# A two-layer transformer block with 64 experts on one core: in the last layer, rows reach the experts and return by matrix products on chip

## What is computed

```python
def moe_ffn(h, router_w, router_bias, w_gu, w_down, shared_gu, shared_down):
    scores = jax.nn.sigmoid(jnp.dot(h, router_w))
    _, idx = lax.top_k(scores + router_bias, TOP_K)                # 6 of 64 experts for each token
    gates = jnp.take_along_axis(scores, idx, axis=-1)
    gates = gates / jnp.sum(gates, axis=-1, keepdims=True) * ROUTED_SCALE
    ...
    # for each expert e, on the rows of the tokens that chose it:
    #   y = (silu(rows @ w_gu[e][:, :384]) * (rows @ w_gu[e][:, 384:])) @ w_down[e]     times the gate
    return routed + swiglu(h, shared_gu, shared_down)
...
xl = xl + mod_l[5] * y
```

## Time and profile before

| what | before |
|---|---|
| median of 3 runs | 2591.6 us (2590.67 to 2595.17) |
| the profiled execution's span, first to last instruction | 2591.4 us |
| experts of the last layer: first weight transfer issued | 1766.44 us |
| span left after the stretch in which the transfers run without a break | 2535 us to the end |
| TensorE busy | 2249.8 us (87%) |
| DVE, ACT, GpSimd busy | 740.5, 417.0, 311.3 us |

### The profile page before, as it was taken

The page is one execution under the profiler, slowest core; times in us unless marked ns, Lnnn a source line. Parts: engine busy times, 40 slices in busy tenths (PEclk is TensorE's granted clock), DMA queues, the critical chain, the costliest instruction groups (busy, mean ns, idle before and its releaser), DMA issues. The chain is left out here.

```text
span 2591.4 us, 40524 instructions
## 1 busy us (share of the span) xinstructions
PE 2249.8 (87%) x17039; PEld 1151.1 (44%) x17039; DVE 740.5 (29%) x1653; ACT 417.0 (16%) x886; POOL 311.3 (12%) x368
## 2 busy tenths in 40 slices
PE   6999899999778797888888999898978889888887
PEld 2457644454333343434434557655433334343333
DVE  2365655371011011111115466645201101011112
ACT  2322344110000000000001333431000000000000
POOL 0007200011111111110000007100111101000000
PEclk8999999999989999999999999999998999999999
DMA  8000297279999999999988100136999999999994
GB/s 326 33 17 35 92 377 291 115 286 394 426 424 406 421 409 419 417 416 383 397 356 343 41 31 6 71 117 259 373 426 414 417 415 421 417 418 412 416 419 198
DMA packets 96345, 780.92 MB, mean 301 GB/s; under 512 B 21736, under 2 KB 22136, under 8 KB 37280
## 3 DMA queue, kind: packets, MB, share of 16 engines
q1 hardware_dynamic: 74848, 740.46, 69.7%
q0 software_dynamic: 21312, 37.81, 3.9%
HBM read 772.55 MB, written 41.29 MB: 314 GB/s over the span
## 5 line engine op out<-in xcount | busy, mean ns | idle before, releaser
L1513 PE MATMUL banks<-arena,htreg 128*32 128x384 f32 (+2 forms) x5824 | 879.4, 533 | 199.6 <-DMA arena<-in_exp_w_gu 194.3
L1513 PEld LDWEIGHTS banks<-arena,htreg 128*32 128x32 f32 (+2 forms) x5824 | 403.4, 137 | 648.7 <-issue 507.3
L1538 PE MATMUL banks<-arena,modreg 128*32 128x512 f32 (+2 forms) x2184 | 400.0, 598 | 40.5 <-issue 37.8
L2314 DVE TENSOR_TENSOR modreg<-modreg,banks 128x384 f32<-128x384 f32 x74 | 40.9, 553 | 1029.8 <-ACT modreg L1831 1029.8
L1538 PEld LDWEIGHTS banks<-arena,modreg 128*32 128x32 f32 (+2 forms) x2184 | 137.6, 127 | 250.4 <-issue 247.8
L1064 PE MATMUL banks<-arena,htreg 128*128 128x512 f32 (+3 forms) x480 | 159.0, 490 | 0.0
L2466 DVE COPY modreg<-banks 128x512 f32<-128x512 f32 x68 | 47.0, 691 | 318.9 <-PE banks L1538 318.9
L1837 ACT ACTIVATE modreg<-banks 128x384 f32<-128x384 f32 x74 | 36.3, 490 | 550.5 <-PE banks L1529 550.5
L2629 POOL DMA_INDIRECT y_d<-modreg,lst x68 | 67.5, 992 | 455.4 <-DVE modreg L2466 454.5
L1064 PEld LDWEIGHTS banks<-arena,htreg 128*128 128x128 f32 x480 | 89.7, 191 | 65.0 <-issue 61.0
L1831 ACT ACTIVATE modreg<-banks 128x384 f32<-128x384 f32 x74 | 36.3, 490 | 491.5 <-PE banks L1513 491.5
(11 more groups left out here) (407 smaller groups left out, 2173.6 us busy)
## 6 DMA issues: line engine op xcount, KB each, us to landing
arena<-in_exp_w_gu SPq DMA_DIRECT2D x256, 1536.0 KB
arena<-in_exp_w_down SPq DMA_DIRECT2D x128, 1536.0 KB
arena<-in_w_mod SPq DMA_DIRECT2D x32, 1024.0 KB, 11.4
arena<-y_d SPq DMA_DIRECT2D x6, 3072.0 KB, 16.7
modreg<-in_w_mod SPq DMA_DIRECT2D x14, 1024.0 KB, 8.3
modreg<-mod_d SPq DMA_DIRECT2D x20, 512.0 KB
arena<-in_shared_w_gu SPq DMA_DIRECT2D x6, 1536.0 KB
arena<-in_w_in SPq DMA_DIRECT2D x4, 2048.0 KB, 12.5
```

Of the source, the lines that this page charges most:

```text
L1513: last = mm(gu_bank(n, half)[rows, 0:DE], src[:, k, rows], up4[q][:, i, DE * half:DE * (half + 1)], start=(k == 0), stop=(k == KD - 1))
L1538: last = mm(ps[4 + half][rows, :], actT[:, k, rows], dn3[q][:, k, 512 * half:512 * half + 512], start=(k == 0), stop=(k == KE - 1))
L2314: tt(act_, sgb, gu_bank(n, 1)[:, 0:DE], ALU.mult).then_inc(unit_act.sem, 1)
```

## The change

In the last layer, nothing of a unit's rows passes through HBM any more. `places` holds for each token and each of the 100 groups of 32 slots the slot that the token has there; comparing it with 0..31 gives a one-hot matrix (`one_hot`), and the product of the token rows with it gives the unit's rows, already transposed (`gather_by_product`). The results return by the product with the transposed one-hot matrix, scaled with the gates (`gate_rows`, `gates_of`, `combine`), which DVE adds to an accumulator of all 256 tokens (`added`). The lists, the gathers, the scatters and the final reading of `y_d` go. Experts of few tokens share a unit by fours (32 slots each); there are 25 routed units (`LAST_CAPS`: 4 experts may have 128 slots, 4 have 96, 16 have 64 and 40 have 32). The second pass stays for rows beyond these slots, and is skipped as a whole when there are none. The first layer keeps its way.

```diff
+LAST_CAPS = ((4, 4), (4, 3), (16, 2), (40, 1))
+    whole = [[(u, i) for i in range(4)] for u in range(4)]
+    big = [[(u, 0), (u, 1), (u, 2), (67 - u, 0)] for u in range(4, 8)]
+    pair = [[(r, 0), (r, 1), (r + 1, 0), (r + 1, 1)] for r in range(8, 24, 2)]
+    quad = [[(r + i, 0) for i in range(4)] for r in range(24, 60, 4)]
...
+            for i, quad in enumerate(units[3]):
+                order.append(quad)
+                if i < 4:
+                    order += [units[0][i], units[2][i]]
+                elif i < 8:
+                    order += [units[1][i - 4], units[2][i]]
...
+                        experts[n] = [sp.value_load(eid[0:1, eid_at[l][r]:eid_at[l][r] + 1], min_val=0, max_val=NE - 1)
+                                      for r in WORK[l][n][1]]
...
+                def gather_by_product(n):
...
+                    for k in range(KD):
+                        for j in range(2):
+                            rows = h[:, 2 + j, :].rearrange("p (d k) -> p k d", k=KD)
+                            last = mm(ps[k // 4][:, tok(k % 4)], rows[:, k, :], hot[r % 2][:, j, :], start=(j == 0), stop=(j == 1))
+                def gate_rows(n):
...
+                    for i in range(4):
+                        column = perm[:, 4 * u + i:4 * u + i + 1].broadcast_to([NE, 32])
+                        last = mm(gu_bank(n, 0)[32 * i:32 * i + 32, :], column, by_expert, start=True, stop=True)
+                def combine(n, j):
...
+                    for half in range(2):
+                        if j and n < NW[l] - 1:
+                            pe.wait_ge(comb_added.sem, comb_added.at(0, 4 * r + half + 1))
+                        mm(comb_bank(n, j, half), gated[r % 2][:, P * j:P * j + P], outs[r % 2][:, 512 * half:512 * half + 512],
+                           start=True, stop=True).then_inc(comb_psum.sem, 1)
...
+                    for n in range(EARLY, NW[l] + 1):
+                        if n < NW[l]:
+                            unit_part(n, "lo")
+                        act_transposed(n - 1)
+                        if n > EARLY:
+                            gate_rows(n - 1)
+                        if n < NW[l]:
+                            unit_part(n, "hi")
+                        if n >= EARLY + 2:
+                            combine(n - 2, 0)
+                        if n + 1 < NW[l]:
+                            gather_by_product(n + 1)
+                        if n >= EARLY + 2:
+                            combine(n - 2, 1)
+                        unit_down(n - 1)
...
+                        tt(gated[r % 2], gated[r % 2], bank[:, SEQ:2 * SEQ], ALU.mult).then_inc(gated_ready.sem, 1)
...
+                            tt(acc_last[:, j, cols], acc_last[:, j, cols], gu_bank(n + 1, half)[:], ALU.add).then_inc(comb_added.sem, 1)
...
+                if l == LAST:
+                    more_last(pool, pool_more, zeros_and_lists)
+                    break
```

More of the change, by code:

```diff
@@ L369, in build @@
         RING = 4
[L370 removed]
+        eid = sb("eid", [P, max(NE, N_COL)], U32)
         lst1 = sb("lst1", [P, max(UNITS)], U32)
@@ L719, in heads4, with more_last, meet @@
             return ap.rearrange("p t (g d) -> p t g d", d=d)
+        def more_last(eng, body, before=None, after=None):
+            n_phase = phases["last"]
+            met = [n_phase - 1]
+            def meet():
+                met[0] += 1
+                eng.drain().then_inc(phase_done.sem, 1)
+                eng.wait_ge(phase_done.sem, 5 * met[0])
+            l = LAST
+            eng.wait_ge(addr_ready.sem, addr_ready.at(l, 1))
+            big = eng.value_load(maxcnt[0:1, 0:1], min_val=0, max_val=NT * P + P)
+            with eng.If(big > P):
+                meet()
+                if before:
+                    before()
+                meet()
+                with eng.Fori(0, R[l]) as r:
+                    with eng.Fori(0, NE // RING) as i:
+                        for b in range(RING):
+                            body(EX[f"more{l}"], l, r, RING * i + b, r * NE + RING * i + b,
+                                 r * (NE // RING) + i, b)
+                if eng is nc.gpsimd:
+                    done = EX[f"more{l}"]["scattered"][0]
+                    eng.wait_ge(done.sem, done.at(l, NE * R[l]))
+                meet()
+                if after:
+                    after()
+                meet()
+            eng.nop()
         def more_slots(eng, name, l, body, gives):
@@ new lines, in _ @@
+                dve.wait_ge(h_ready.sem, h_ready.at(2 * l + 1, n_t))
+                link(dve.memset(mask[:, n_t, :], 0.0))
+                dve.wait_ge(order_act.sem, order_act.after(l, "scores"))
+                link(tt(selb[:, nt_, :], scores[:, nt_, :], bc(srow("rbias"), 1, n_t), ALU.add))
+                for i in range(n_t):
+                    link(dve.max(out=top8[:, i, :], in_=selb[:, i, :]))
+                    link(dve.max_index(out=idx8[:, i, :], in_max=top8[:, i, :], in_values=selb[:, i, :]))
@@ new lines, in _ @@
+                link(ts(unit_hot[lo64, 0:U_], K("experts")[lo64, 0:U_], rankcol[lo64], None, ALU.is_equal))
+                dve.wait_ge(order_psum.sem, order_psum.after(l, "rank"))
+                link(dve.tensor_copy(rank, ps[0][:, 0:NE]))
+                link(ts(shift_by, rank, float(U_), 2.0, ALU.is_ge, ALU.mult))
+                link(stt(shift_by, rank, float(NE - G_), shift_by, ALU.is_ge, ALU.add))
+                link(ts(cap, rank, float(W_), 1.0, ALU.is_lt, ALU.add))
+                for end in (W_ + G_, NE - G_):
+                    link(stt(cap, rank, float(end), cap, ALU.is_lt, ALU.add))
```

575 lines of the change are left out of this document (399 added, 176 removed).

## The result

| | before | changed |
|---|---|---|
| median | 2593.1 us (4 runs, 2590.7 to 2595.2) | 2572.1 us (4 runs, 2570.4 to 2574.8) |
| profiled execution's span | 2591.4 us | 2570.5 us |
| ratio of the times | | 0.992, 95% interval 0.991 to 0.994 |

The change made the kernel 21 us faster, 0.8%. The forecast was 79 us, and its range (2494 to 2548) doesn't hold the result.

A forecast was written before the change was run, and what follows sets the result against it. The prediction took weight transfers to bound the last layer, with PE hidden: flow from 1771.3, plus 720 of stream, 5 of gaps and 16.2 of end, gives 2512 us, 79 less than before; range 2494 to 2548.

The forecast's parts named there:

- PE in a unit: PE's work per routed unit of the last layer: 22.8 us, some 24.5 with hand-overs; 25 units 610 us, hidden under 720.
- Does the ring hold?: Weight buffers of the last layer: PE needs about 42 us against 43, so they hold by a hair; 5 us of gaps.
- tight round: First half of the last layer's order: four-, one- and two-expert unit in turn, four times, with some tenths of gaps each.
- Rival 2: PE's chain in the last layer: two-sided hand-overs make a unit 28 us instead of 24.5; 2544 us, chance 0.10.
- The stream's price: Last layer's weight transfers: 3.75 us for each chunk of 1.573 MB, so 720 us for all 192 chunks.
- The bound from the end's slices: Last layer's weight transfers running alone at 427 GB/s: 3.68 us a chunk, 707 us for the layer.
- Rival 1: Last layer's weight transfers: row traffic was free, so a chunk keeps 3.93 us; 2546 us, chance 0.09.
- Rival 5: Last layer's weight transfers: alone they run at 427 GB/s without gaps, 707 us for 725; 2494 us, chance 0.10.
- The start: Start of the last layer's weight stream: first issue at 1769.2, flow from 1771.3, 2.8 us later than before.
- The end: From the last weight chunk to the kernel's end: 16.2 us in place of 55.4.
- Rival 3: PE in the last layer: clock stays at 1.2 GHz, a unit takes about 42 us; about 2850 us, chance 0.03.
- Rival 4: After the last layer's units: the second pass runs all 64 experts again; about 3950 us, chance 0.02.

The follow-up runs named there:

- e1: Changed kernel with the last layer's h written so that gathering products load contiguous columns, not every eighth value; same result: 2520.4 us, 0.973 of before.
- e3: Changed kernel with each unit's 16 gathering products replaced by eight transposes of contiguous rows, so units work on wrong rows: 2500.1 us, 0.965 of before.
- e4: Kernel before the change, its last layer's indirect gathers and scatters letting only the first row or two through: 2545.4 us, 0.982 of before.
- e8: Changed kernel with contiguous gathering loads and, in each round, the two-expert unit moved to directly behind the four-expert unit: 2513.7 us, 0.970 of before.

## Why the prediction was wrong

**The step that failed** is "PE in a unit". It set the new products at "16 products of the same 128x128 form (0.144 each: 2.3)", the gate rows at 0.45 and the four return products at 1.8, in all 22.8 us a unit, "some 24.5 with six hand-overs". Measured is 28.3 to 28.6 without its waits, 28.4 in what follows. With it failed the step that was built on it, "Does the ring hold?", which puts PE's work in a tight round at 42 us. Two errors made the new products 8.0 us too cheap:

- *Counting.* I took the mean of one record and multiplied it by the number of instructions in the program. But the trace shows each float32 product as two records. The evidence stood in front of me: the down part of a unit in four groups has 48 records in the timeline, where the order of the changed kernel lists 24 products for such a part. Return products are 3.8 us and not 1.8, gate rows 1.06 and not 0.45, and the gathering would be 32 x 0.117 = 3.7 us even without a stride. The Trainium skill, "FP8 and Floating Point Precision", section "TensorE Precision Notes", says that true FP32 needs four passes. The trace agrees in total: a record of 512 columns takes 0.44 us (5.31 / 12 in L1701, at a granted clock of 1.00, 2.4 GHz), so two records are some four cycles a column for one product.
- *The wrong neighbour.* The row of 0.144 us was that of transposes. They had the same stride of every eighth value and hardly showed it; a product does. e1 shows what the stride costs there: 0.239 against 0.117 us a record, 3.9 us a unit. The Trainium skill, "Advanced Engine Details and Errata", section "SBUF Cachelines", states that SBUF has lines of 16 bytes and that access to another line each time pays a penalty. Here the values lie 32 bytes apart, and the trace agrees that there is a penalty; the page gives no figure, and that the lines are its reason is not shown by any run here.

Half of this error was hidden by luck. The other terms were too dear: `lo` and `hi` at 6.1 us each ran at 5.4 (1.5 us), and of the 1.7 us of hand-overs nothing is seen, the groups even overlap by 0.9 us in all. So 24.5 + 8.0 - 1.5 - 1.7 - 0.9 = 28.4.

**Why a unit of 28.4 us costs so much.** 25 x 28.4 = 710 us is still less than the 720 of the stream as forecast (at 3.69 us a chunk it is 708), so by means alone PE would be nearly hidden. But the ring is only eight chunks deep, and units differ in weights, not in PE time. A round of three units takes PE 85.4 us, waits and the slower parts behind them left out. In the first four rounds it needs 21 chunks, 78 us at e3's price: PE sets the pace. In the later ones 24 chunks, 89 us: the stream should. The stretches between the first and the fifth, and the fifth and the eighth four-expert down part:

```profile
1843.56:2202.53 358.97, 348.26 (x1941) 195.07 (x1940) 76.22 (x133) 18.96 (x36) 0.00 (x0) 0.98 0.90 373
2202.53:2484.64 282.11, 263.74 (x1780) 139.88 (x1780) 57.06 (x100) 14.23 (x27) 0.00 (x0) 0.95 0.97 405
```

The first four rounds take 89.7 us each, in place of the forecast's 21 x 3.75 = 78.8: 44 us lost in four rounds, with the DMA share at 0.90. The next three take 94.0 in place of 90: another 12. Together 56, about the 57 us by which the last weights come later than forecast (about 2553 for 2496). In every round PE also waits once, at the four-expert unit, for 2 to 6 us, and then runs one `hi` part in 6.6 to 8.1 us in place of 5.4. So both lose: neither is busy throughout, and the sum is longer than either alone.

The forecast's own check of the ring shows the 11 us of a tight round, once it has the measured parts. It puts the last down part of a four-expert unit 42 us behind the start of its `hi` part, against 43 us of transfers. In the timeline above the `hi` part starts at 2065.34 and the down part ends at 2117.91: 52.6 us, since the products and the gathering, taken as 4.7 us, are 11.1 and 11.0. All transfers that the ring allows are done by then. The DMA rate from 2060 to 2140 us (2 us a slice) is 0 from 2110 to 2118, and SP sends the next chunk when the down part ends:

```profile
GB/s 418 424 455 399 442 438 406 418 412 442 430 424 430 430 428 418 430 436 436 430 401 363 418 289 31 0 0 0 0 98 418 414 387 387 430 430 399 418 406 449
...
2118.12 0.33 SPq L1010 DMA_DIRECT2D arena<-in_exp_w_down  x1
```

**Rival 2** had the right path, PE's chain through the ring, and nearly the right unit, 28 us, but for another reason: it charged the hand-overs, and the timeline shows none; the time is in the products themselves. It priced the unit at 32 us, with six a tight round. It was 11 a tight round: the three units' own sum, 85.4 for 78.8, gives 6.6 of them, and the wait with the slower part behind it the rest (85.4 to 89.7, 4.4 by the waits and parts of the timeline). The first half of the order was where most of it was decided.

**Other steps.**
- The stream's price of 3.75 us a chunk was a little high: e3 and e4 have 3.69 and 3.70. The bound from the end's slices, 3.68, was the right neighbour. The row traffic's cost of 46 us is more than its share of engine time on q0, which is 4.5% of the whole stream of 767.5 us, 34.5 us: the weights' own packets gained too, since q1's share before, 95.7% of 650 us for 165.6 chunks, is 3.76 us of engine time each, 0.06 more than in e4. For 192 chunks that is 11.5 us, and with the 34.5 the 46 are there. *Rival 1* (row traffic was free) is refuted by e4.
- *Rival 5* (427 GB/s without gaps, 2494) is what e3 shows to be there once PE is short enough: 2500.
- The start was right: 2.7 us later, forecast 2.8.
- The end was right: 15.7 us from the start of the last down part, and about 17.5 from the last weights, for 16.2. The last down part ran without a slow start (5.36, taken 7.5), and what stands behind it took 10.4 us in place of 8.7.
- *Rival 3* (the clock at 1.2 GHz throughout) did not come. The granted clock between 1850 and 2500 us rose from 0.93 to 0.97, and PE was busy for 620.9 us in place of 548.0. The work after a wait ran slower, as in the rows of before, and all else at 5.4 us.
- *Rival 4* did not come: nothing follows the last unit.

With the unit that I had worked out, the time would have been near the forecast: e1, whose unit is 24.4 us (2050.76 to 2075.11, down part to down part) with the same order and ring, came to 2520 us against 2512 forecast. That is shown. It is in part luck that it is so near: e1 takes 20 us more than e3, where the forecast has 5 us of gaps for such a unit, and the stream's price, 11.5 us too high, covers most of the difference. That e1's unit is just the forecast one is chance too, as e1 takes away the stride and not the double records. That the two errors are the whole difference is not shown by a run of its own; it follows from e1 and from the account above. What stays open is how much of the 4.4 us of wait and slow start in each round a deeper ring would take away, and what the better order of e8 would give with the stride left in; neither was tried.

## What to carry to other kernels

Count the records that the trace shows for an instruction before you multiply its mean by the program's count; and price a new matmul from a row of the same operation and the same access pattern, not only of the same shape: a transpose with the same stride didn't show what the stride costs a product. Where a ring of few buffers joins two engines, compare them round by round: the time is the sum of the larger of the two in each round and something for the change-over, not the larger of the two sums. And a layout that costs nothing in one place (rows with a stride, for transposes) may cost 50 us once a product reads it on the path.

## What the runs showed of the hardware

- A float32 product is two records of the trace, a float32 transpose one.
- A float32 product with a stationary operand of every eighth value (32 bytes apart) takes 0.239 us a record of 128 columns, with contiguous values 0.117. A transpose takes 0.144 with this stride and 0.130 without.
- Weight transfers of 1.5 MB take 3.93 us with indirect row transfers of 10.47 MB in 650 us beside them (own share 4.5%), and 3.70 where nearly as many packets of these carry 0.10 MB in 600 us (0.8%).
- Return products of 32 columns cost a third of those of 512 (29.9 against 96.3 us for 200 records), not a sixteenth: 0.15 us each, in groups of four.
- After waits of 2 to 6 us for weights a part of 5.37 us took 6.6 to 8.1 us. In one of them, 7.89 us from 2065.34, the granted clock was 0.67.
